# An earlier start behind four normalisations of a two-layer decoder step: what moves on each engine

## The chip, the core and the metric

The kernel runs on one core of one Trainium2 chip, as a single program. The metric is the device time of one execution in microseconds (us). Engines and the names that the profile gives them: TensorE (PE for its matmuls, PEld for its weight loads), VectorE (DVE), ScalarE (ACT), GpSimd (POOL) and SyncE (SP), which issues the weight transfers. The engines run side by side, each in its own program order, and wait for each other by semaphores only.

## The reference, cut to what matters

256 prompt tokens and 8 sample tokens go through two layers together, so that every operand has 264 columns. All sub-layers have the same frame:

```python
x = LayerNorm(alpha * x + (1 + gate) * sublayer(x * (1 + scale) + shift))
# layer 0: q, k, v = h @ w_qkv; attention; @ w_o      then  (silu(h @ w1) * (h @ w3)) @ w2
# layer 1: a, g = h @ w_pw1 + b; u = a * sigmoid(g); depthwise conv over 31 taps;
#          silu(layernorm(.)) @ w_pw2 + b             then  top-2-of-8 mixture of experts
```

`LayerNorm` takes mean and variance over the 1024 channels. `scale`, `shift` and `gate` are rows of `silu(c) @ ada_w + ada_b`, one vector per sequence. Everything is float32.

## The kernel before, in words

Activations lie transposed: 128 partitions hold 128 channels, eight chunks of them (`KC` = 8) make the 1024 channels, and the columns are the 264 tokens. A float32 product is made of three passes: both operands are cut into a high part (`w_hi`, `h_hi`, a cast to the rounded type `fp32r` on ScalarE) and a low part (`w_lo`, `h_lo`, the difference, on VectorE), and TensorE adds hi*hi, hi*lo and lo*hi.

**Weights.** SyncE loads blocks of 1 MB into a ring of seven slots, in the order of the list `stream`. A block of 1024 rows by 256 columns is split in two units; ScalarE casts a unit (line 982), VectorE subtracts (line 1245). There is room for two split blocks (`SPLITS` = 4 units), so a block is split only when the block two places before it has been used: `freed` holds the count of filled banks that says so (line 473). `split_behind(name)` splits the block two places behind `name`; the place of the call in VectorE's and ScalarE's program decides when.

**Dense stages.** `dense` (line 459) takes one block after the other. Each block makes two groups of 24 matmuls (8 chunks by 3 passes), one group in one bank of 512 floats. Six banks go round: `group()` lets TensorE wait until the group six places before it has been drained by VectorE (`psum_drained`). The stages are q/k/v (12 blocks "qkv"), the output product ("wo", 4), "f1"/"f3" (11 pairs), "f2", "p1"/"p1g" (4 pairs) and "p2" (4). Behind them the mixture of experts runs through its own loops.

**Norms.** `norm` of TensorE, ScalarE and VectorE together: VectorE adds the residual chunk by chunk, TensorE sums the chunks into the mean, VectorE centres in four parts (line 1326), ScalarE squares each part (line 969), TensorE sums the squares, ScalarE takes the root (line 971) and VectorE the reciprocal (line 1329). Norms 0 (behind wo), 1 (behind f2), 2 (inside the convolution module), 3 (behind p2) and 4 (at the end). `norm_modulate` then makes the next operand `hT` in two halves of four chunks, ScalarE casts each half to `h_hi` (line 995) and VectorE subtracts `h_lo` (line 1256). After both, `h_ready` is announced, and the next dense stage waits for that.

**Beside the norms.** TensorE is given other work while it waits: in norms 0, 1 and 2 it multiplies four pieces of `ada_w` each (`ada_rows`, line 485), whose four groups are the four that stand in front of the next stage's groups in the round of banks. VectorE copies them out (`ada_row`, line 1212) behind `h_ready` (behind `conv_ready` in norm 2), and TensorE turns them into columns behind the first blocks of the next stage (`ada_turn`, line 497).

**First stage.** For qkv VectorE splits block 0, makes `hT` (`modulate`), and then splits block 1.

## Time and profile before

| what | value |
|---|---|
| time of the runs | 2003.96 us median of 3 (2002.76 to 2003.96) |
| the profiled execution | 2008.72 us, its span 2007.0 us |
| TensorE busy | 1831.6 us (91%) |
| VectorE busy | 1524.6 us (76%) |
| ScalarE busy | 1168.8 us (58%) |
| DMA | 579 MB, mean 289 GB/s |

The span runs from the first to the last instruction; the time of the execution has 1.7 us around it. The first 755 us of the span are the stages that the change touches, the rest is the mixture of experts and norm 4. A busy share is an average over stages with different limits: what counts for the change are the places where TensorE stands still at a stage's border.

### The profile page before, as it was taken

How to read it: one execution, taken by the hardware profiler on the slowest of the kernel's cores; microseconds unless marked ns; L12 is line 12 of the kernel's file. 1: busy time of each engine (PE TensorE's matmuls, PEld its weight loads, DVE VectorE, ACT ScalarE, POOL GpSimd, SP SyncE). 2: the span in 40 equal slices, each digit the busy share in tenths (PEclk: the TensorE clock that was granted, in tenths of full speed). 3: DMA queues.
4: the chain of work that ended last, by engine and by line, in shares of the span. 5: the costliest groups of instructions: out<-in, count | busy, mean ns of one | idle time of the engine just before them, and what ended most of it. 6: DMA issues, size and time to landing. Idle time of an engine off the chain costs nothing.

```text
span 2007.0 us, 27233 instructions
## 1 busy us (share of the span) xinstructions
PE 1831.6 (91%) x10086; PEld 1471.7 (73%) x10086; DVE 1524.6 (76%) x1604; ACT 1168.8 (58%) x1030; POOL 18.1 (1%) x73
## 2 busy tenths in 40 slices
PE   5999778999899878998999999999999999999997
PEld 2974457999788766676676767676688787887885
DVE  2567736555679758989899898989888788887884
ACT  1321213443345327888877887877767767676773
POOL 2000000000000000000000000000000000000000
PEclk8985778999989888999999999999999999999998
DMA  9747677555743416999999999999999899898980
GB/s 299 230 149 238 245 251 252 168 174 182 240 141 104 175 39 245 382 385 388 388 390 394 380 388 386 381 386 390 387 330 366 324 338 370 304 357 337 329 314 22
DMA packets 246105, 579.27 MB, mean 289 GB/s; under 512 B 10478, under 2 KB 122550, under 8 KB 246013
## 3 DMA queue, kind: packets, MB, share of 16 engines
q1 hardware_dynamic: 245005, 573.98, 78.7%
q0 software_dynamic: 1024, 4.25, 0.6%
q8 instruction: 51, 0.84, 0.2%
q14 instruction: 25, 0.20, 0.0%
HBM read 574.79 MB, written 4.35 MB: 289 GB/s over the span
## 4 chain that ended last, share of the span: by engine, by line
PE 58%; DVE 16%; issue 7%; ACT 5%; DVEq 1%; DMA 0%; ACTq 0%; SPq 0%; PEldq 0%
PE banks L861 17%; PE banks L468 12%; DVE w_lo L1622 12%; PE banks L849 11%; PE banks L819 4%; ACT w_hi L1092 4%; PE banks L678 3%; PE banks L699 2%; PE banks L805 1%; PE banks L765 1%; PE banks L783 1%; PE banks L540 1%; PE banks L517 1%; PE banks L829 1%; PE banks L497 1%
## 5 line engine op out<-in xcount | busy, mean ns | idle before, releaser
L1622 DVE TENSOR_TENSOR w_lo<-ring,w_hi 128x2048 fp32r<-128x2048 f32 x420 | 945.6, 2288 | 146.0 <-ACT w_hi L1092 146.0
L1092 ACT CAST w_hi<-ring 128x2048 fp32r<-128x2048 f32 x420 | 798.7, 1912 | 265.9 <-PE banks L861 169.1
L861 PE MATMUL banks<-w_hi,x_s 128*128 128x512 f32 x672 | 279.3, 416 | 45.5 <-DVE w_lo L1622 39.6
L849 PE MATMUL banks<-w_hi,g_buf 128*128 128x512 f32 x784 | 282.5, 401 | 5.2 <-DVE w_lo L1622 2.8
L861 PE MATMUL banks<-w_hi,x_m 128*128 128x512 f32 x896 | 283.1, 392 | 2.3 <-DVE w_lo L1622 2.3
L468 PE MATMUL banks<-h_hi,w_hi 128*128 128x264 f32 x800 | 238.1, 298 | 29.5 <-DVEq L430 29.5
L861 PE MATMUL banks<-w_lo,x_s 128*128 128x512 f32 x672 | 264.7, 394 | 0.0
L982 ACT CAST w_hi<-ring 128x1024 fp32r<-128x1024 f32 x124 | 121.5, 1031 | 198.3 <-PE banks L468 93.0
L468 PE MATMUL banks<-h_lo,w_hi 128*128 128x264 f32 x800 | 233.9, 292 | 0.0
L468 PE MATMUL banks<-h_hi,w_lo 128*128 128x264 f32 x800 | 233.4, 292 | 0.0
L1245 DVE TENSOR_TENSOR w_lo<-ring,w_hi 128x1024 fp32r<-128x1024 f32 x124 | 143.9, 1204 | 106.0 <-ACT w_hi L982 105.2
L849 PE MATMUL banks<-w_lo,g_buf 128*128 128x512 f32 x560 | 218.9, 391 | 0.0
L861 PEld LDWEIGHTS banks<-w_hi,x_s 128*128 128x128 f32 x672 | 127.0, 189 | 113.7 <-DVE w_lo L1622 86.4
L861 PEld LDWEIGHTS banks<-w_hi,x_m 128*128 128x128 f32 x896 | 168.2, 188 | 37.6 <-DVE w_lo L1622 2.7
L849 PEld LDWEIGHTS banks<-w_hi,g_buf 128*128 128x128 f32 x784 | 147.2, 188 | 53.1 <-DVE w_lo L1622 22.4
L468 PEld LDWEIGHTS banks<-h_hi,w_hi 128*128 128x128 f32 x800 | 158.4, 198 | 31.5 <-DVEq L430 31.2
L861 PE MATMUL banks<-w_lo,x_m 128*128 128x512 f32 x448 | 174.5, 389 | 0.0
L468 PEld LDWEIGHTS banks<-h_lo,w_hi 128*128 128x128 f32 x800 | 158.5, 198 | 0.4
L468 PEld LDWEIGHTS banks<-h_hi,w_lo 128*128 128x128 f32 x800 | 157.4, 197 | 0.0
L861 PEld LDWEIGHTS banks<-w_lo,x_s 128*128 128x128 f32 x672 | 127.3, 189 | 23.7
L849 PEld LDWEIGHTS banks<-w_lo,g_buf 128*128 128x128 f32 x560 | 105.3, 188 | 19.8
L861 PEld LDWEIGHTS banks<-w_lo,x_m 128*128 128x128 f32 x448 | 84.1, 188 | 17.1
(347 smaller groups left out, 1912.8 us busy)
## 6 DMA issues: line engine op xcount, KB each, us to landing
ring<-in_moe_w_dram SPq DMA_DIRECT2D x420, 1024.0 KB, 7.4
ring<-in_ada_w_dram SPq DMA_DIRECT2D x48, 1024.0 KB, 5.9
ring<-in_ffn_w_dram SPq DMA_DIRECT2D x30, 1024.0 KB, 5.5
ring<-in_attn_w_qkv_dram SPq DMA_DIRECT2D x12, 1024.0 KB, 11.9
ring<-in_conv_w_pw_dram SPq DMA_DIRECT2D x12, 1024.0 KB, 9.7
ring<-in_cache_k_dram SPq DMA_DIRECT2D x16, 512.0 KB, 6.0
ring<-in_cache_v_dram SPq DMA_DIRECT2D x16, 512.0 KB, 7.5
ring<-in_attn_w_o_dram SPq DMA_DIRECT2D x4, 1024.0 KB, 8.5
```

What stands on the lines that cost most here:

```text
L468: mm = pe.matmul(bk[:, 0:T], w, x[:, k, :], start=(k == 0 and i == 0), stop=(k == KC - 1 and i == 2))
L497: mm = pe.matmul(bk[:, 9 * m:9 * m + 9], arow[i % 4][:, m * P:(m + 1) * P], fold, start=True, stop=True)
L517: mm = pe.matmul(stat[:, 0:T], mean_w[:, :], z[:, c, :], start=(c == 0), stop=(c == KC - 1))
L678: mm = pe.matmul(two[m][:, 0:T], w, x[:, g, :], start=(g == 0 and i == 0), stop=(g == FM - 1 and i == 2))
L699: mm = pe.matmul(bk[:, 0:TP], dw_diag[:, (c * PE_TAPS + i) % DIAGS, :], up[:, c, j:j + TP], start=(i == 0), stop=(i == PE_TAPS - 1))
L819: mm = pe.matmul(t_b[:, b, i * SMALL:(i + 1) * SMALL], h_rows[:, b, i * P:(i + 1) * P], joint[:, :], start=True, stop=True)
L849: mm = pe.matmul(out_b[:, b, :], g, y, start=(p == 0 and t == 0 and i == 0), stop=(p == NCH - 1 and t == 2 * last + 1 and i == len(g_passe ...
L861: mm = pe.matmul(bk[:, b, :], x, y, start=(k == 0 and i == 0), stop=(k == KC - 1 and i == len(x_passes(k, hi, lo)) - 1), skip_group_check= ...
L982: act.copy(w_hi[:, (q * UNITS + u) % SPLITS, 0:e - o], ring[:, n % RING, o:e]).then_inc(ev("w_hi_ready"), 1)
L1092: act.copy(w_unit(n)[0], ring[:, pos_of(n), :]).then_inc(ev("moe_hi_ready"), 1)
L1245: dve.tensor_tensor(w_lo[:, i, 0:e - o], ring[:, n % RING, o:e], w_hi[:, i, 0:e - o].bitcast(F32), ALU.subtract).then_inc(ev("w_lo_ready"), 1)
L1622: dve.tensor_tensor(lo, ring[:, pos_of(n), :], hi.bitcast(F32), ALU.subtract).then_inc(ev("moe_lo_ready"), 1)
```

## The change

Four edits, in TensorE's, ScalarE's and VectorE's programs. The numbers of lines in the diff are those of the two files; the rows named L487, L1267, L1278, L1234, L1349 and so on are the changed file's names for what is L468, L1245, L1256, L1212, L1326 before.

1. A new function `dense_halves` multiplies two blocks at once: it waits for both split blocks, takes all four groups, and then does the first four chunks for all groups, and the last four for all groups. It waits for `h_lo_ready` of each half in place of `h_ready`. It is used for qkv 0 and 1, f1/f3 0, p1/p1g 0 and p2 0 and 1. Both blocks count as used when all four groups are filled.
2. In norms 0 and 1 the last split in front of the centring is moved behind the centring on VectorE (`split_behind(behind)` in `rstd_ready`).
3. ScalarE takes a root of one column (`warm`) in front of the squares of every norm, which places the root's table load there.
4. In `modulate` (qkv) the low part of half 0 is made inside half 1, as `norm_modulate` does already.

```diff
+            def dense_halves(i, slots, x_hi, x_lo, behind=None):
+                for s in slots:
+                    wait_split(s)
+                groups = [(s, m, group((s, m))) for s in slots for m in range(2)]
+                for half in range(2):
+                    pe.wait_ge(ev("h_lo_ready"), 2 * i + half + 1)
+                    for s, m, bk in groups:
+                        for k in range(4 * half, 4 * half + 4):
+                            hi, lo = halves(s, k, m)
+                            for n, (w, x) in enumerate(((hi, x_hi), (hi, x_lo), (lo, x_hi))):
+                                mm = pe.matmul(bk[:, 0:T], w, x[:, k, :], start=(k == 0 and n == 0),
+                                               stop=(k == KC - 1 and n == 2), skip_group_check=True)
+                        if half:
+                            filled(mm)
+                for s in slots:
+                    freed[split_no[s]] = (psum_filled, len(order))
+                if behind is not None:
+                    for s, m, _bk in groups:
+                        behind(s, m)
...
-            pe.wait_ge(ev("h_ready"), 1)
-            dense([("qkv", j) for j in range(12)], h_hi, h_lo)
+            dense_halves(0, [("qkv", j) for j in range(2)], h_hi, h_lo)
+            dense([("qkv", j) for j in range(2, 12)], h_hi, h_lo)
...
-            pe.wait_ge(ev("h_ready"), 2)
-            for j in range(FF // 256):
+            dense_halves(1, [("f1", 0), ("f3", 0)], h_hi, h_lo)
+            while pending:
+                ada_turn()
+            for j in range(1, FF // 256):
                 dense([("f1", j), ("f3", j)], h_hi, h_lo)
...
-                dense([("p1", j), ("p1g", j)], h_hi, h_lo)
-                if j == 0:
+                if j:
+                    dense([("p1", j), ("p1g", j)], h_hi, h_lo)
+                else:
+                    dense_halves(2, [("p1", j), ("p1g", j)], h_hi, h_lo)
...
-            pe.wait_ge(ev("conv_ready"), 2)
             behind = mean_behind(3, zT)
-            dense([("p2", 0)], h_hi, h_lo, behind)
+            dense_halves(3, [("p2", 0), ("p2", 1)], h_hi, h_lo, behind)
             while pending:
                 ada_turn()
-            dense([("p2", j) for j in range(1, 4)], h_hi, h_lo, behind)
+            dense([("p2", j) for j in range(2, 4)], h_hi, h_lo, behind)
...
             def norm(i, z, s):
+                act.activation(warm[:, 0:1], eps_t[:, 0:1], ACT.Sqrt)
                 for part in range(PARTS):
...
             def low_halves(i, half):
-                step(dve.tensor_tensor(h_lo[:, c, :], hT[:, c, :], h_hi[:, c, :].bitcast(F32), ALU.subtract))
+                step(dve.tensor_tensor(h_lo[:, c, :], hT[:, c, :], h_hi[:, c, :].bitcast(F32), ALU.subtract), ev("h_lo_ready"))
...
             def modulate(i, layer, k):
                 for half in range(2):
                     s = slice(4 * half, 4 * half + 4)
+                    if half:
+                        low_halves(i, 0)
...
-                for half in range(2):
-                    low_halves(i, half)
+                low_halves(i, 1)
                 announce("h_ready")
...
-            def rstd_ready(i, z):
+            def rstd_ready(i, z, behind=None):
...
+                if behind is not None:
+                    split_behind(behind)
                 dve.wait_ge(ev("ln_std_ready"), i + 1)
...
-                if c % 2:
+                if c % 2 and c < KC - 1:
                     split_behind(("wo", c // 2))
-            norm_modulate(0, zT[:, :, :], PRM_LNG, PRM_LNB, 1, beside_norm[0])
+            norm_modulate(0, zT[:, :, :], PRM_LNG, PRM_LNB, 1, beside_norm[0], ("wo", 3))
...
-                split_behind(("f2", cb, 2))
-            norm_modulate(1, zT[:, :, :], PRM_LNG + KC, PRM_LNB + KC, 2, beside_norm[1])
+                if cb < 3:
+                    split_behind(("f2", cb, 2))
+            norm_modulate(1, zT[:, :, :], PRM_LNG + KC, PRM_LNB + KC, 2, beside_norm[1], ("f2", 3, 2))
...
-                if c == 1:
+                if c == 3:
                     while pending:
                         ada_turn()
```

**VectorE, the first stage** (`hT` and `h_lo` for qkv; the two `w_lo` rows at the end are block 1). In the words behind each row stand the semaphores it waits for. Before:

```order
L1245 TENSOR_TENSOR w_lo<-ring,w_hi 128x1024 [waits w_hi_ready] x2
L1264 TENSOR_SCALAR hT<-xT,adaT 128x256 [waits psum_drained]
...
L1268 TENSOR_TENSOR hT<-t,adaT 128x4x8 [waits vector_step]
L1264 TENSOR_SCALAR hT<-xT,adaT 128x256 [waits vector_step]
...
L1256 TENSOR_TENSOR h_lo<-hT,h_hi 128x1056 [waits vector_step,h_hi_ready]
L1256 TENSOR_TENSOR h_lo<-hT,h_hi 128x1056 [waits h_hi_ready]
L1245 TENSOR_TENSOR w_lo<-ring,w_hi 128x1024 [waits vector_step,w_hi_ready]
```

Now:

```order
L1267 TENSOR_TENSOR w_lo<-ring,w_hi 128x1024 [waits w_hi_ready] x2
L1288 TENSOR_SCALAR hT<-xT,adaT 128x256 [waits psum_drained]
...
L1278 TENSOR_TENSOR h_lo<-hT,h_hi 128x1056 [waits vector_step,h_hi_ready]
L1288 TENSOR_SCALAR hT<-xT,adaT 128x256 x4
...
L1278 TENSOR_TENSOR h_lo<-hT,h_hi 128x1056 [waits vector_step,h_hi_ready]
L1267 TENSOR_TENSOR w_lo<-ring,w_hi 128x1024 [waits h_lo_ready,w_hi_ready]
L1267 TENSOR_TENSOR w_lo<-ring,w_hi 128x1024 [waits w_hi_ready]
```

The low part of half 0 now stands in front of the second half's work; block 1's split is still last.

**VectorE, norm 0** (from the last residual chunk to the copies of the `ada_w` rows). Before:

```order
L1317 TENSOR_TENSOR zT<-zT,t 128x8 [waits psum_drained,vector_step,ln_chunk_ready]
L1245 TENSOR_TENSOR w_lo<-ring,w_hi 128x1024 [waits w_hi_ready] x2
L1326 TENSOR_TENSOR zT<-zT,banks 128x528 [waits stats_filled,ln_chunk_ready]
L1326 TENSOR_TENSOR zT<-zT,banks 128x528 x3
L1329 RECIPROCAL rstd<-std 128x264 [waits ln_std_ready]
...
L1256 TENSOR_TENSOR h_lo<-hT,h_hi 128x1056 [waits vector_step,h_hi_ready]
L1212 COPY arow_sb<-banks 128x512 [waits vector_step,psum_filled]
L1212 COPY arow_sb<-banks 128x512 [waits psum_drained,psum_filled]
```

Now:

```order
L1340 TENSOR_TENSOR zT<-zT,t 128x8 [waits psum_drained,vector_step,ln_chunk_ready]
L1349 TENSOR_TENSOR zT<-zT,banks 128x528 [waits stats_filled,ln_chunk_ready]
L1349 TENSOR_TENSOR zT<-zT,banks 128x528 x3
L1267 TENSOR_TENSOR w_lo<-ring,w_hi 128x1024 [waits w_hi_ready] x2
L1354 RECIPROCAL rstd<-std 128x264 [waits ln_std_ready]
...
L1278 TENSOR_TENSOR h_lo<-hT,h_hi 128x1056 [waits vector_step,h_hi_ready]
L1234 COPY arow_sb<-banks 128x512 [waits h_lo_ready,psum_filled]
L1234 COPY arow_sb<-banks 128x512 [waits psum_drained,psum_filled]
```

The split is behind the centring; the copies of the `ada_w` rows stand behind the second `h_lo`, as before.

**TensorE, the start of f1/f3 0** (the row in front is the last of the `ada_w` rows). Before:

```order
L485 MATMUL banks<-ring,cT_sb 32x256 [waits slot2_loaded]
L485 MATMUL banks<-ring,cT_sb 32x256 x7
L468 MATMUL banks<-h_hi,w_hi 128x264 [waits psum_drained,w_lo_ready,h_ready]
...
L468 MATMUL banks<-h_hi,w_hi 128x264 [waits psum_drained]
...
L468 MATMUL banks<-h_hi,w_hi 128x264 [waits psum_drained,w_lo_ready]
```

Now:

```order
L507 MATMUL banks<-ring,cT_sb 32x256 [waits slot2_loaded]
L507 MATMUL banks<-ring,cT_sb 32x256 x7
L487 MATMUL banks<-h_hi,w_hi 128x264 [waits psum_drained,h_lo_ready,w_lo_ready]
L487 MATMUL banks<-h_lo,w_hi 128x264
...
L487 MATMUL banks<-h_hi,w_hi 128x264 [waits h_lo_ready]
```

The waits for drained banks, which stood in front of each of the four groups, stand in front of the very first matmul now; 48 matmuls later only the second half of `h_lo` is waited for.

## Rows read from the trace of the kernel before

**Rows 1.** The page's head: the span.

```profile
span 2007.0 us, 27233 instructions
```

**Rows 2.** TensorE's waits from 25 to 1999 us: for whom, total, times, longest.

```profile
PE banks L468 <- DVEq L430: 29.5, 5, 9.1
...
PE banks L642 <- DMA ring<-in_cache_v_dram: 5.2, 1, 5.2
...
PE banks L712 <- DMA arena<-in_state_conv_dram: 3.8, 1, 3.8
```

**Rows 3.** Timeline, first stage: start, duration, engine, line, tiles, [idle before <- releaser].

```profile
46.73 1.38 DVE L1264 TENSOR_SCALAR hT<-xT,adaT 128x256 f32<-128x256 f32 x4
...
48.52 1.07 ACT L995 CAST h_hi<-hT 128x1056 fp32r<-128x1056 f32 x1
...
50.44 2.43 DVE L1256 TENSOR_TENSOR h_lo<-hT,h_hi 128x1056 fp32r<-128x1056 f32 x2
52.98 0.29 PEld L468 LDWEIGHTS banks<-h_hi,w_hi 128*128 128x128 f32 x1 [9.17 <-DVEq L430]
```

**Rows 4.** Timeline of VectorE and ScalarE: splits of block qkv 1 and of a later one.

```profile
53.01 2.36 DVE L1245 TENSOR_TENSOR w_lo<-ring,w_hi 128x1024 fp32r<-128x1024 f32 x2
...
67.45 2.00 ACT L982 CAST w_hi<-ring 128x1024 fp32r<-128x1024 f32 x2 [3.79 <-PE banks L468]
68.53 2.36 DVE L1245 TENSOR_TENSOR w_lo<-ring,w_hi 128x1024 fp32r<-128x1024 f32 x2 [0.70 <-ACT w_hi L982]
```

**Rows 5.** Timeline, norm 0, from the last split to the root.

```profile
306.01 1.83 PE L517 MATMUL banks<-zT,mean_w 128*128 128x264 f32 x6
...
306.26 1.99 ACT L982 CAST w_hi<-ring 128x1024 fp32r<-128x1024 f32 x2 [4.70 <-PE banks L468]
...
309.62 2.54 DVE L1326 TENSOR_TENSOR zT<-zT,banks 128x528 f32<-128x528 f32 x4
310.35 2.49 ACT L969 ACTIVATE arena<-zT 128x528 f32<-128x528 f32 x4 [2.09 <-DVE zT L1326]
...
312.86 1.28 ACT L971 ACT_TABLE_LOAD   x1
...
314.91 0.48 ACT L971 ACTIVATE std<-banks,eps_t 128x264 f32<-128x264 f32 x1 [0.77 <-PE banks L540]
```

**Rows 6.** Timeline, mixture of experts: another table load and a small activation behind it.

```profile
745.62 1.28 ACT L1102 ACT_TABLE_LOAD   x1
...
746.91 0.20 ACT L1102 ACTIVATE edif<-dif 128x3 f32<-128x3 f32 x1
```

**Rows 7.** Timeline, norm 0, the low parts and the copies behind them.

```profile
321.77 1.26 DVE L1256 TENSOR_TENSOR h_lo<-hT,h_hi 128x1056 fp32r<-128x1056 f32 x1
...
325.85 1.26 DVE L1256 TENSOR_TENSOR h_lo<-hT,h_hi 128x1056 fp32r<-128x1056 f32 x1 [1.19 <-ACT h_hi L995]
...
327.25 1.53 DVE L1212 COPY arow_sb<-banks 128x512 f32<-128x512 f32 x2
```

**Rows 8.** The chain that ended last, in order of time, behind norm 0.

```profile
327.22 13.84 PE banks L468 x96
341.06 3.47 PE banks L497 x32
```

**Rows 9.** Timeline of VectorE: one product of the f stage; the copies in norm 2.

```profile
339.04 0.42 DVE L1510 TENSOR_TENSOR arena<-arena,banks 128x264 f32<-128x264 f32 x1
...
685.43 1.53 DVE L1212 COPY arow_sb<-banks 128x512 f32<-128x512 f32 x2
```

**Rows 10.** Stretches: start:end, us, busy of each engine, granted PE clock, DMA share, GB/s.

```profile
344.60:348.60 4.00, 4.00 (x22) 4.00 (x22) 1.90 (x7) 0.00 (x0) 0.00 (x0) 0.58 0.51 146
...
562.80:566.70 3.90, 0.11 (x1) 0.00 (x0) 2.93 (x5) 3.75 (x5) 0.00 (x0) 1.00 0.39 98
570.30:577.10 6.80, 6.80 (x34) 6.80 (x33) 1.83 (x7) 0.42 (x2) 0.00 (x0) 0.50 0.58 188
577.10:581.00 3.90, 3.90 (x20) 3.90 (x20) 3.68 (x9) 0.00 (x0) 0.00 (x0) 0.53 0.02 4
```

More of the change, by code:

```diff
@@ L132, in build @@
         std = sb("std", [P, T])
+        warm = sb("warm", [P, 1])
         rstd = sb("rstd", [P, T])
@@ L657, in _ @@
             norm(0, zT, sq, beside=beside_norm[0])
-            pe.wait_ge(ev("h_ready"), 2)
-            for j in range(FF // 256):
+            dense_halves(1, [("f1", 0), ("f3", 0)], h_hi, h_lo)
+            while pending:
+                ada_turn()
+            for j in range(1, FF // 256):
                 dense([("f1", j), ("f3", j)], h_hi, h_lo)
-                if j == 0:
-                    while pending:
-                        ada_turn()
             behind = mean_behind(1, zT)
@@ L689, in _ @@
             norm(1, zT, sq, beside=beside_norm[1])
-            pe.wait_ge(ev("h_ready"), 3)
             def taps(c):
@@ L705, in _ @@
             for j in range(4):
-                dense([("p1", j), ("p1g", j)], h_hi, h_lo)
-                if j == 0:
+                if j:
+                    dense([("p1", j), ("p1g", j)], h_hi, h_lo)
+                else:
+                    dense_halves(2, [("p1", j), ("p1g", j)], h_hi, h_lo)
                     pe.wait_ge(ev("state_loaded"), 32)
@@ L1281, in fuse, with norm_modulate @@
                 step(dve.tensor_tensor(fuse_b[:, :, :], fuse_b[:, :, :], shift, ALU.add))
-            def norm_modulate(n, z, g, b, i, beside=()):
-                rstd_ready(n, z)
+            def norm_modulate(n, z, g, b, i, beside=(), behind=None):
+                rstd_ready(n, z, behind)
                 for half in range(2):
```

## The prediction

> **What bounds the kernel now.** I read the page's head first: a span of 2007.0 us [rows 1], inside an execution of 2008.72 us. Then the waits of TensorE, because it is the engine that is busy for 91%: between its work it waited 29.5 us in five places for the next dense operand, the longest 9.1 us [rows 2]. Those are the borders that the change aims at. Each is read in the timeline. The chain of waits shows what comes behind a border: 96 matmuls in 13.84 us without a hole, and four column turns in 3.47 us [rows 8], with the next block right behind them. So inside the stages TensorE is the bound, and what a border gains or loses runs through to the end; I found no later stage that waits for a fixed moment. For the change three things must be followed at each border: when the first matmul may start, when the two blocks' room is free again, and what the clock does.
>
> **First stage (qkv): later start.** In the changed order the first matmul needs both blocks' low parts, and block 1's subtractions still stand behind the making of the operand. Half of `hT` is made from 46.73 to the cast at 48.52, 1.79 us; the cast takes 1.07, a low part 2.43/2 = 1.22 [rows 3]. Now VectorE must wait for the cast before it goes on: low part 0 is done at 48.52 + 1.07 + 0.03 + 1.22 = 50.84, half 1 is made by 52.63, its cast by 53.70, low part 1 by 54.95. Then come block 1's subtractions, 0.14 + 2.36 us [rows 4]: 57.45, and TensorE starts at 57.5 and not at 52.98 [rows 3]. That is **+4.5**. The early low part helps nobody, because the weights come last.
>
> **First stage: an empty room.** `dense_halves` frees both blocks only when all four groups are full, so that block 2 can be split only then. Before, block 0's room came free 48 matmuls earlier and this was hidden. A split takes 67.45 to 68.53 + 2.36 = 70.89, 3.44 us [rows 4]; with an estimated 0.3 for the hand-over at both ends TensorE stands still for **+3.75**. Ends: 3.44 with no hand-over, and 4.2 if VectorE's copies of the groups come in between.
>
> **The clock behind such a hole.** The granted clock was still 1.00 in a wait of 3.9 us and 0.50 in the work behind it; that is the 2.4 and the 1.2 GHz level [rows 10]. Behind the column turns of norm 0 it was 0.58 over 4.0 us: 84% of them at the lower level, half of which is lost, 1.7 us [rows 10]. In the hole of 3.75 us I expect the same: **+1.7** (ends 0 and 2.0). Together +9.95 for qkv.
>
> **Norm 0: the squares.** Without the split in front, the centring could start some 1.7 us earlier, when the mean is there (the sums end at 306.01 + 1.83 = 307.84, the centring started at 309.62 [rows 5]). But ScalarE is late then. Its last cast ends at 308.25, the table load takes 1.28, and the small root, which the trace does not have, lies between 0 and the 0.48 of the whole root [rows 5]; I take the 0.20 of the nearest small activation [rows 6]. The squares start at 309.75 and not at 310.35: **-0.6** (ends -0.8 and -0.3). The load as such wins nothing: after it ScalarE waited another 0.77 us for TensorE's sums [rows 5], and that pause is the same in all norms. In norms 2, 3 and 4 nothing stands in front of the centring, ScalarE has time for the load: 0. VectorE's moved 2.36 us end near 313, before the root at 314.3: hidden; without that cover they would cost up to 2.36. They free a ring slot 3 us later, so that the last pieces of `ada_w` land later; TensorE has some 7 us of waiting to take them.
>
> The Trainium skill, "ScalarE: Activation LUTs", section "What ACT_TABLE_LOAD costs", gives a load of 1283 ns and a drain of about 1380 ns more, 2.66 us a switch. The load agrees with the trace (1.28), the drain does not: the next activation starts at 746.91, right behind the load that ends at 746.90 [rows 6]. By the page's figure the squares of norms 0 and 1 would start 1.38 us later than I say.
>
> **Norms 0, 1 and 2: the start behind the copies.** The early start needs the first low part alone, at 323.03 and not 327.11 in norm 0 [rows 7]. It will not come. All four groups are taken in front of the first matmul, there are six banks, and the four groups before them are the `ada_w` rows. Group 4 needs the bank of the second row, and VectorE copies the rows behind the second low part: two copies, 1.53 us, from 327.25 [rows 7]. So TensorE starts at 327.25 + 1.53 + 0.07 = 328.85, or 328.25 with the 0.6 gained, against 327.22 [rows 8]: **+1.05**. Norm 1 has the same copies and the same order in front of them, so the same gain: **+1.05**. Part of that could hide in the wait of 3.8 us for the conv state [rows 2], but VectorE's four splits behind p1g 0 move with the end of the blocks and hold its copies for the next turns; I count it whole (ends 0 and 1.05). Norm 2 has the copies [rows 9] and no gain: **+1.6**. For p2 the room is no trouble: two mean sums and four column turns fill the 3.7 us in which block 2 is split. Ends for that: 0 and +0.7.
>
> **f1/f3 behind norm 0.** The pair ends 13.84 us after its start, as before. Before, f1 1 was split while f3 0 was multiplied, and only the turns (3.47) stood between [rows 8]. Now ScalarE casts f1 1 from the end on; after 0.2 + 3.44 us VectorE has its low part, and only behind it stand the two products of 0.42 [rows 9], after which the four banks are handed back: about 4.7 us. Turns 3 and 4 need these banks. So f1 1 starts 4.7 + 3.47/2 = 6.5 us behind the end at full clock; the clock will have fallen by then, which makes the two turns 3.5 us long: 8.2 us, against 3.47, **+4.75**. The low level then lasts some 4 us from the start of the full matmuls, as it did behind the turns of norm 1 (0.53 over 3.9 us [rows 10]), and costs 2.0 in place of 1.7: **+0.3**. Ends for the two: +3.0 and +5.5. In p1 the next splits waited for both blocks anyway: 0.
>
> **The sum.** 4.5 + 3.75 + 1.7 + 1.05 + 4.75 + 0.3 + 1.05 + 1.6 = 18.7 us. The profiled execution took 2008.72, and would be 2027.4; the median of the runs is 2003.96, 4.8 below it, and the steps are waits between engines, the same in both. So 2003.96 + 18.7 = **2022.7 us**.
>
> **The rivals.**
> - *The clock stays up* in the qkv hole and in turns 3 and 4. For: a fall needs its moment, and the hole is no longer than the one in which it had not yet fallen. Against: it fell right behind it. Without 1.7 + 1.75 + 0.3 it is +14.95: 2018.9.
> - *Later waits swallow a part.* The wait of 5.2 us for the V pages [rows 2] could be a transfer that comes at its own time; then a later qkv stage costs that much less: +13.5, 2017.5. Against: the pages are asked for when ring slots come free, and these move along.
> - *The table switch holds ScalarE 2.66 us*, as the activations in front of the squares would then: 2 x 1.38 more, +21.5, 2025.4. Against it stands the row above. The page named above is its source.
> - *Faster: TensorE starts with the first low part everywhere.* Place: the first matmul of the four stages. Start at 50.9 in qkv (-2.0), 4.1 + 0.6 earlier in norms 0 and 1, 3.1 in norm 2: -14.5; the holes stay (3.75 + 1.7 + 3.0 = +8.45): -6, 1998. It decides once three of the four starts come at the first `h_lo`. For: that is how the code reads. Against: the waits for block 1 and for the banks in the order of the instructions.
> - *Nothing to be seen*: losses at the holes are hidden by slack that I missed, and the sum is under 4 us.
>
> **Chances and range.** The forecast 0.60, with a range of its own from 2020 to 2026; clock up 0.17; swallowed 0.08; table switch 0.05; more than summed (copies in the holes, 2027 to 2030) 0.04; faster 0.03; no change 0.03. The range from 2016 to 2027 takes in the first four with most of their spread. A measurement of this kernel tells about 0.2% (4 us) from no change. Faster 0.03, same 0.03, slower 0.94.
>
> **What would show it.** In the changed profile: first matmul of qkv at about 57.5; a hole of 3.5 to 4 us in TensorE between qkv 1 and qkv 2, then matmuls at double spacing; squares of norm 0 starting 0.6 us earlier against the last cast; the first matmul behind norms 0, 1 and 2 right behind the second copy of an `ada_w` row; a hole between the second and third turn behind f1/f3 0, and the next block 8 us behind the pair. I am wrong if one of these starts follows the first low part, if a stage's end catches up what its start lost, or if the attention stage takes less time than before.

## The result and the profile after

The changed kernel took **2032.04 us** (median of 4 runs, 2030.67 to 2036.5), the kernel before 2003.96 beside it: a ratio of 1.0133, 95% interval 1.0117 to 1.0149, which is +26.7 us (23.4 to 29.9). It is slower, as forecast, but the forecast of 2022.7 us is 9.3 us too low and its range ended at 2027.

The profiled execution took 2031.49 us. Its head answers to [rows 1]:

```profile
span 2029.7 us, 27245 instructions
```

TensorE's waits of the changed kernel (for whom, total, times, longest) answer to [rows 2]:

```profile
PE banks L487 <- DVE arow_sb L1234: 17.4, 3, 8.0
PE banks L487 <- DVE w_lo L1267: 13.3, 1, 13.3
...
PE banks L664 <- DMA ring<-in_cache_v_dram: 5.0, 1, 5.0
...
PE banks L469 <- DVE w_lo L1267: 3.6, 1, 3.6
...
PE banks L519 <- DVEq L416: 2.8, 1, 2.8
```

The 29.5 us in five places have become 17.4 behind the copies of `ada_w` rows (three places: norms 0, 1, 2), 13.3 in front of qkv behind block 1's subtractions, and two new holes, 3.6 and 2.8. No start stands behind a low part. TensorE's waits for pieces of `ada_w` grew from 3.4 to 10.0 us, but they fall into time in which it would wait anyway: in norm 0 the last piece is done at 325.54, three microseconds before its row can be copied.

**First stage**, timeline of the changed kernel, against [rows 3, 4]:

```profile
49.94 1.07 ACT L1017 CAST h_hi<-hT 128x1056 fp32r<-128x1056 f32 x1 [1.68 <-DVEq L431]
...
56.60 2.36 DVE L1267 TENSOR_TENSOR w_lo<-ring,w_hi 128x1024 fp32r<-128x1024 f32 x2
59.03 0.29 PEld L487 LDWEIGHTS banks<-h_hi,w_hi 128*128 128x128 f32 x1 [13.39 <-DVE w_lo L1267]
...
73.04 3.89 ACT L1004 CAST w_hi<-ring 128x1024 fp32r<-128x1024 f32 x4 [17.88 <-PE banks L487]
74.12 2.36 DVE L1267 TENSOR_TENSOR w_lo<-ring,w_hi 128x1024 fp32r<-128x1024 f32 x2 [3.63 <-ACT w_hi L1004]
...
76.53 0.39 PE L469 MATMUL banks<-h_hi,w_hi 128*128 128x264 f32 x1 [3.59 <-DVE w_lo L1267]
```

From the first `h_hi` to TensorE's first load it is 9.09 us against 4.46, and block 2 comes 3.59 us after the pair. The stretch behind that hole (columns as in [rows 10]) has the lower clock level again:

```profile
76.90:80.40 3.50, 3.50 (x20) 3.50 (x19) 2.52 (x3) 0.03 (x1) 0.00 (x0) 0.53 0.76 257
```

**Norm 0**, timeline, against [rows 5]:

```profile
307.91 1.82 PE L539 MATMUL banks<-zT,mean_w 128*128 128x264 f32 x6
308.17 1.99 ACT L1004 CAST w_hi<-ring 128x1024 fp32r<-128x1024 f32 x2 [4.70 <-PE banks L469]
...
309.85 2.55 DVE L1349 TENSOR_TENSOR zT<-zT,banks 128x528 f32<-128x528 f32 x4 [0.87 <-PE banks L539]
310.18 1.28 ACT L987 ACT_TABLE_LOAD   x1
311.47 0.20 ACT L987 ACTIVATE warm<-eps_t 128x1 f32<-128x1 f32 x1
311.58 2.23 ACT L991 ACTIVATE arena<-zT 128x528 f32<-128x528 f32 x4
312.31 2.35 DVE L1267 TENSOR_TENSOR w_lo<-ring,w_hi 128x1024 fp32r<-128x1024 f32 x2
316.13 0.48 ACT L993 ACTIVATE std<-banks,eps_t 128x264 f32<-128x264 f32 x1 [2.31 <-PE banks L562]
```

From the start of the last cast to the start of the squares: 3.41 us against 4.09. The centring starts right behind the mean, but ScalarE is late by the load. The moved subtractions end at 314.66, before the root at 316.13.

**The start and the hole behind norm 0**, against [rows 7, 8]:

```profile
327.13 1.26 DVE L1278 TENSOR_TENSOR h_lo<-hT,h_hi 128x1056 fp32r<-128x1056 f32 x1 [1.19 <-ACT h_hi L1017]
328.54 1.53 DVE L1234 COPY arow_sb<-banks 128x512 f32<-128x512 f32 x2
330.32 0.56 PE L487 MATMUL banks<-h_hi,w_hi 128*128 128x264 f32 x1 [4.78 <-DVE arow_sb L1234]
...
343.33 1.85 PE L519 MATMUL banks<-fold,arow_sb 128*128 128x9 f32 x16
343.58 1.99 ACT L1004 CAST w_hi<-ring 128x1024 fp32r<-128x1024 f32 x2 [2.43 <-PE banks L487]
344.77 2.36 DVE L1267 TENSOR_TENSOR w_lo<-ring,w_hi 128x1024 fp32r<-128x1024 f32 x2 [10.16 <-ACT w_hi L1004]
347.05 0.76 DVE L1535 TENSOR_TENSOR arena<-arena,banks 128x264 f32<-128x264 f32 x2
348.01 3.55 PE L519 MATMUL banks<-fold,arena 128*128 128x9 f32 x16 [2.83 <-DVEq L416]
...
351.41 0.57 PE L469 MATMUL banks<-h_hi,w_hi 128*128 128x264 f32 x1
```

All of that is near what was forecast. What was not is the mixture of experts, whose code the change does not touch. From its first cast of weights to the squares of norm 4 it takes 1246.84 us (765.22 to 2012.06), before 1235.66 (753.46 to 1989.12). In each matmul there the operand of 128 columns that is loaded first (`x_s` or `x_m`, the experts' tokens, or `g_buf`, their gated product) is called stationary, and the weights of 512 columns (`w_hi`, `w_lo`) are the moving operand. These matmuls before (duration in ns: min/median/max, first and last start in us):

```profile
L861 PE MATMUL banks<-w_hi,x_m x896: 387/389/587, 1455.3 to 1950.4; 128*128 128x512 f32 x180
L861 PE MATMUL banks<-w_lo,x_s x672: 387/389/628, 766.7 to 1433.8; 128*128 128x512 f32 x168
...
L849 PE MATMUL banks<-w_hi,g_buf x784: 387/389/504, 812.4 to 1973.3; 128*128 128x512 f32 x196
```

and after:

```profile
L882 PE MATMUL banks<-w_hi,x_m x896: 387/396/588, 1468.1 to 1973.1; 128*128 128x512 f32 x180
L882 PE MATMUL banks<-w_lo,x_s x672: 387/395/628, 778.5 to 1446.6; 128*128 128x512 f32 x168
...
L870 PE MATMUL banks<-w_hi,g_buf x784: 392/396/502, 824.3 to 1996.4; 128*128 128x512 f32 x196
```

The same instructions are some 6 ns longer (only those of `w_hi` with `x_s`, whose median was 393 before, by 3). The clock is not the cause, it is 1.00 in both. The experts' stretch, before:

```profile
770.00:1985.00 1215.00, 1153.70 (x5265) 899.68 (x5265) 1040.96 (x648) 912.02 (x588) 0.00 (x0) 1.00 0.94 354
```

and after:

```profile
781.00:2008.00 1227.00, 1170.97 (x5265) 901.27 (x5264) 1043.32 (x649) 914.40 (x590) 0.00 (x0) 1.00 0.93 351
```

5265 matmuls (some 4000 of them of this kind) are busy for 17.3 us more, the stretch is 12 us longer, and VectorE, ScalarE and the weight loads are busy for as long as before within 2.5 us. Up to the first `x_m` matmul the stage costs only +1.0 us, because TensorE waits for VectorE's splits there and its waits shrink instead (41.9 us to 39.4, the row L861 or L882 behind `w_lo`); behind it TensorE is the bound and it costs +10.1. In the chain of waits the same 72 matmuls stand with 16.38 us before and 16.79 after.

### The profile page after: what moved, and what is told of

Its sections match the earlier page's. It is cut to its first block, busy times and chain, and to the rows that moved or that the text cites. A ratio compares the mean times of both kernels' runs of the same rounds, so it can differ in the third digit from the quotient of the medians.

```text
span 2029.7 us, 27245 instructions
## 1 busy us (share of the span) xinstructions
PE 1843.8 (91%) x10086; PEld 1472.5 (73%) x10086; DVE 1525.7 (75%) x1604; ACT 1169.0 (58%) x1035; POOL 18.2 (1%) x73
## 4 chain that ended last, share of the span: by engine, by line
PE 58%; DVE 16%; issue 7%; ACT 5%; DVEq 1%; DMA 0%; ACTq 0%; SPq 0%; PEldq 0%
PE banks L882 17%; DVE w_lo L1648 11%; PE banks L870 11%; PE banks L469 10%; PE banks L840 4%; ACT w_hi L1114 3%; PE banks L699 3%; PE banks L719 2%; PE banks L487 2%; PE banks L826 1%; PE banks L786 1%; PE banks L804 1%; PE banks L562 1%; PE banks L539 1%; PE banks L519 1%
## 5 line engine op out<-in xcount | busy, mean ns | idle before, releaser
L882 PE MATMUL banks<-w_hi,x_s 128*128 128x512 f32 x672 | 281.0, 418 | 41.7 <-DVE w_lo L1648 37.2
L882 PE MATMUL banks<-w_hi,x_m 128*128 128x512 f32 x896 | 288.6, 398 | 2.3 <-DVE w_lo L1648 2.3
L882 PE MATMUL banks<-w_lo,x_s 128*128 128x512 f32 x672 | 267.1, 397 | 0.0
L1267 DVE TENSOR_TENSOR w_lo<-ring,w_hi 128x1024 fp32r<-128x1024 f32 x124 | 143.8, 1204 | 118.2 <-ACT w_hi L1004 117.5
L882 PEld LDWEIGHTS banks<-w_hi,x_s 128*128 128x128 f32 x672 | 127.0, 189 | 111.8 <-DVE w_lo L1648 82.6
L469 PE MATMUL banks<-h_hi,w_hi 128*128 128x264 f32 x672 | 197.7, 294 | 4.2 <-DVE w_lo L1267 3.6
L882 PEld LDWEIGHTS banks<-w_hi,x_m 128*128 128x128 f32 x896 | 168.3, 188 | 42.9 <-DVE w_lo L1648 2.7
L469 PE MATMUL banks<-h_lo,w_hi 128*128 128x264 f32 x672 | 194.7, 290 | 0.0
L469 PE MATMUL banks<-h_hi,w_lo 128*128 128x264 f32 x672 | 194.5, 289 | 0.0
L882 PE MATMUL banks<-w_lo,x_m 128*128 128x512 f32 x448 | 177.1, 395 | 0.0
L882 PEld LDWEIGHTS banks<-w_lo,x_s 128*128 128x128 f32 x672 | 127.4, 190 | 25.1
L469 PEld LDWEIGHTS banks<-h_hi,w_hi 128*128 128x128 f32 x672 | 131.3, 195 | 4.8 <-DVE w_lo L1267 3.8
L469 PEld LDWEIGHTS banks<-h_lo,w_hi 128*128 128x128 f32 x672 | 131.2, 195 | 0.3
L469 PEld LDWEIGHTS banks<-h_hi,w_lo 128*128 128x128 f32 x672 | 130.5, 194 | 0.0
L882 PEld LDWEIGHTS banks<-w_lo,x_m 128*128 128x128 f32 x448 | 84.2, 188 | 19.9
```

The lines of the kernel that those rows point to most:

```text
L469: mm = pe.matmul(bk[:, 0:T], w, x[:, k, :], start=(k == 0 and i == 0), stop=(k == KC - 1 and i == 2))
L882: mm = pe.matmul(bk[:, b, :], x, y, start=(k == 0 and i == 0), stop=(k == KC - 1 and i == len(x_passes(k, hi, lo)) - 1), skip_group_check= ...
L1267: dve.tensor_tensor(w_lo[:, i, 0:e - o], ring[:, n % RING, o:e], w_hi[:, i, 0:e - o].bitcast(F32), ALU.subtract).then_inc(ev("w_lo_ready"), 1)
```

## The experiments

The suspect for the experts was the one thing that the change does to them: `warm`, a new tile of 4 bytes a partition (the line that allocates it is not in the excerpt of the diff above; e2's diff takes it out again). In the program's addresses, which no trace shows, it takes 32 bytes, and all tiles allocated later lie 32 bytes higher, among them `x_s`, `x_m` and `g_buf`. The weights `w_hi` and `w_lo` lie in front of it and stay. Ratios are to the kernel before beside the same runs, with 95% intervals; in us they are taken of its medians there (2004.65 for the first four, 2005.64 for e5 to e8, 2005.23 for e9 to e12, 2002.4 for the last three).

| run | what it is | us, runs | ratio |
|---|---|---|---|
| e1_pad32 | before + unused 4-byte tile | 2018.25, 6 | 1.0061 [1.0048, 1.0074] |
| e2_after_inplace | the change, no tile moved | 2023.63, 6 | 1.0090 [1.0075, 1.0105] |
| e3_no_qkv | e2, qkv as before | 2014.12, 5 | 1.0044 [1.0030, 1.0057] |
| e4_split_only | only the moved splits | 2002.61, 12 | 0.9990 [0.9979, 1.0001] |
| e5_pad64 | before + two such tiles | 2018.48, 4 | 1.0064 [1.0042, 1.0085] |
| e6_pad_x | before, 32 B at the experts' tiles alone | 2015.95, 5 | 1.0049 [1.0032, 1.0066] |
| e7_pad_behind | the 32 B behind them | 2005.75, 1 | |
| e8_split_warm | e4 + the early root | 2005.58, 12 | 0.9996 [0.9983, 1.0009] |
| e9_lazy_own | halves with late banks, own release | 1995.24, 6 | 0.9955 [0.9939, 0.9970] |
| e10_lazy_only | e9, common release | 2000.51, 10 | 0.9978 [0.9967, 0.9990] |
| e11_no_f1 | e2, f1/f3 0 as before | 2018.11, 4 | 1.0058 [1.0038, 1.0078] |
| e12_pad128 | 128 B in front of `x_s` | 2014.04, 1 | |
| e13_pad256 | 256 B in front of `x_s` | 2003.89, 1 | |
| e14_pad_w128 | 128 B in front of `w_hi` | 2005.78, 1 | |
| e15_pad_g128 | 128 B in front of `g_buf` | 2013.23, 1 | |

### The tile

**e1_pad32** puts the tile, unused, into the kernel before; **e2_after_inplace** keeps the whole change but lets the small root write into a free column of `prm`.

```diff
         std = sb("std", [P, T])
+        pad = sb("pad", [P, 1])
```
```diff
-        warm = sb("warm", [P, 1])
+        warm = prm[:, 508:509]
```

> The kernel before with one unused tile of 4 bytes per partition where the change has its tile warm; the tiles behind it then lie 32 bytes further on. Layout theory: the matmuls of the mixture of experts go from a median of 389 to 396 ns, as in the changed kernel, and the time rises by about 11 us (2015). Rival (the mixture of experts was slower for a cause of the run, or of the new order in front of it): the time stays within 3 us of before and the median at 389 ns.

> The changed kernel with the one-column root written into a free column of the parameter tile, so that no tile moves; nothing else differs. Layout theory: median of the expert matmuls back at 389 ns, the time about 11 us below the changed kernel, 12 to 17 us above before (2016 to 2021). Rival (the order causes the slower experts): as the changed kernel, 28 us above before.

The unused tile alone makes the kernel 12.2 us slower (9.6 to 14.8), and the experts' stage 1248.55 us long. Without the shift the whole change costs 18.0 us (15.0 to 21.0), and the experts are back at 1235.56. That is the missing part and the forecast part, each by itself; they add up to 30.2, against 26.7 (23.4 to 29.9) measured. For e1 I had expected about 11; for e2 12 to 17, which is a microsecond below what came.

**Which tiles, and which distance.** e5 adds two tiles; e6 and e7 put the 32 bytes at the experts' tiles, in front of all three or behind them; e12 and e13 widen e6's gap to 128 and 256 bytes.

```diff
+        pad = sb("pad", [P, 8], at=moe)     # e6; e12: [P, 32], e13: [P, 64]
         x_s = sb("x_s", [P, KC, 2, SMALL], F32R, at=moe)
...
         g_buf = sb("g_buf", [P, 2, SLOTW], F32R, at=moe)
+        pad = sb("pad", [P, 8], at=moe)     # e7 alone, in place of the first
```

> The kernel before with two unused tiles of 4 bytes: each takes 32 bytes, so that everything behind them lies 64 bytes further on. If the expert matmuls care where their operand lies within 64 bytes, it is as before: median 389 ns, time within 3 us of before. If they care for the tile's being there, or for 128 bytes and more: 395 ns or over and 10 to 14 us slower.

> The kernel before with 32 bytes put in front of x_s, so that only the experts' tiles (x_s, x_m, g_buf and those behind) move by 32 bytes, and all others stay. If the place of the experts' operands is the cause: 395 ns or more and 10 to 14 us slower, all of it in the mixture of experts. If a tile in front of them is (rstd, the arena): as before.

> The 32 bytes put behind g_buf: x_s, x_m and g_buf, the stationary operands of the expert matmuls, stay on their 64-byte places, and h_rows, the selectors and all others move. If the stationary operands alone count: median 389 ns and the experts' stage 1236 us, as before. If h_rows or another of the moved tiles counts: the 8 to 12 us are there again.

> The kernel before with 128 bytes in front of x_s, so that the experts' tiles move by 128 bytes (e6 moved them by 32). If the stationary operands want to begin on a multiple of 128 bytes: median 389 ns, experts' stage 1236 us. If it is their place as such, or multiples of 256 with an offset of 128: 395 ns or more and 1247 us.

> The kernel before with 256 bytes in front of x_s. If only the place within 256 bytes counts (before, x_s, x_m and g_buf lie 128 bytes past a multiple of 256): median 389 ns, experts' stage 1236 us. If the period is 512 bytes or more, or any move slows: 392 ns or more and 1245 us or more.

Experts' stage: e5 1250.27, e6 1246.83, e7 1235.74, e12 1245.94, e13 1235.79 us. So it is the place of `x_s`, `x_m` and `g_buf` that counts, and not the count of tiles or those behind. 32, 64 and 128 bytes are slow, 256 are as none. The matmuls of `g_buf` in e12 and in e13:

```profile
L850 PE MATMUL banks<-w_hi,g_buf x784: 388/395/506, 807.6 to 1980.2; 128*128 128x512 f32 x196
...
L850 PE MATMUL banks<-w_hi,g_buf x784: 387/389/504, 807.4 to 1968.5; 128*128 128x512 f32 x196
```

**Absolute or relative?** **e14_pad_w128** moves the weights and the token operands together by 128 bytes, **e15_pad_g128** moves `g_buf` alone.

```diff
+        pad = sb("pad", [P, 32])            # e14
         w_hi_all = sb("w_hi", [P, WBUF * SLOTW], F32R)
...
+        pad = sb("pad", [P, 32], at=moe)    # e15 alone
         g_buf = sb("g_buf", [P, 2, SLOTW], F32R, at=moe)
```

> 128 bytes in front of w_hi, so that the moving operands (w_hi, w_lo) and the stationary ones (x_s, x_m, g_buf) move together by 128. If their distance from each other counts: median 389 ns and 1236 us, as before. If the absolute place of the stationary operand counts: as e12, 392 ns or more and 1245 us.

> 128 bytes between x_m and g_buf. If each matmul is slowed by the place of its own stationary operand: the matmuls of w1 and w3 (x_s, x_m) keep 389 ns and those of w2 (g_buf) go to 393, the stage by about 4 us. If the slowing is one for the whole stage: both groups alike.

With all moved together (e14) the stage takes 1235.63 us (of its six groups of matmuls only `w_lo` with `x_s` is off, 393 ns in place of 389; why is open), and the same matmuls:

```profile
L850 PE MATMUL banks<-w_hi,g_buf x784: 387/389/504, 809.4 to 1970.4; 128*128 128x512 f32 x196
```

With `g_buf` alone moved (e15):

```profile
L862 PE MATMUL banks<-w_hi,x_m x896: 387/389/587, 1457.2 to 1954.6; 128*128 128x512 f32 x180
...
L850 PE MATMUL banks<-w_hi,g_buf x784: 390/396/506, 813.4 to 1977.9; 128*128 128x512 f32 x196
```

Only the matmuls that load the moved tile are slow, and the stage takes 1239.18, +3.5. (The run as a whole is longer by more, because its attention stage took 170.6 us and e13's 164.3: more on that below.) So the time of these matmuls depends on the distance in a partition between their two operands: fast where it is what it was or 256 bytes more, slow at 32, 64 or 128 bytes more. Nor is it shown for other shapes: the 528 matmuls of f2, 264 columns wide, whose moving operand `g_hi_f` or `g_lo_f` also lies behind the tile (its chunks are 1056 bytes apart, so they stand at many distances in both), are busy for 150.2 us before and 150.2 in e1.

### The borders

**e3_no_qkv** and **e11_no_f1** take the new order out of one stage each, both on top of e2.

```diff
-            dense_halves(0, [("qkv", j) for j in range(2)], h_hi, h_lo)
-            dense([("qkv", j) for j in range(2, 12)], h_hi, h_lo)
+            pe.wait_ge(ev("h_ready"), 1)
+            dense([("qkv", j) for j in range(12)], h_hi, h_lo)
```
```diff
-            dense_halves(1, [("f1", 0), ("f3", 0)], h_hi, h_lo)
+            pe.wait_ge(ev("h_ready"), 2)
+            dense([("f1", 0), ("f3", 0)], h_hi, h_lo)
```

(e3 also makes `h_lo` of half 0 at its old place.)

> As e2, but the qkv stage as before (dense, low parts behind both halves). If the start of qkv and the hole behind it cost what they cost at their place (11 us at the end of the qkv stage) and the attention stage's later catching up is tied to them: about 2 us below e2. If the catching up has a cause of its own (the clock's phase, the layout of the attention tiles): about 11 us below e2, or the attention stage is as long as before.

> The change in place (no tile moved) with f1/f3 0 as before. My sum: the later start of 1.05 and the hole with its low clock, 5.05, go away: 6.1 us below e2 (2017). Rival (later stages catch up what f1/f3 lost): within 2 us of e2.

Taking the order out of qkv gives back 9.5 us between the medians of e2 and e3 (9.95 in the sum): the second of the two cases that I had named for e3. Taking it out of f1/f3 0 gives 5.5 (1.05 + 4.75 + 0.3 = 6.1 forecast; e11 was timed in another group of runs than e2). By the intervals of the ratios each of the two differences is uncertain by 4 to 5 us, so they agree with the sum but don't prove its terms; the rows do that below.

**e4_split_only** keeps of the change only the splits behind the centring, **e8_split_warm** that and the early root (in place).

```diff
 # e8; e4 is without this line
+                act.activation(warm[:, 0:1], eps_t[:, 0:1], ACT.Sqrt)
```

> The kernel before with nothing but the weight subtractions of norms 0 and 1 moved behind the centring. The centring starts when the mean is there: 1.6 us a norm, -3.2 us in all (2000.8). Rival: the subtractions hold up the reciprocal, or the ring slots freed later hold up the ada_w pieces: no change or slower.

> As e4 (subtractions behind the centring), and the one-column root in front of the squares of every norm, in place, so that no tile moves. My sum: in norms 0 and 1 the squares wait for ScalarE's table load and start 1.0 us later than in e4, nothing in the other norms: +2.0 us against e4. Rival (the early table load gains 1.28 us a norm): 2 to 6 us below e4.

The squares start 2.42 us behind the last cast in e4, 3.41 in e8, as in the changed kernel. Norm 0 of e4, where the table load is behind the squares again:

```profile
302.97 1.83 PE L539 MATMUL banks<-zT,mean_w 128*128 128x264 f32 x6
...
304.91 2.55 DVE L1349 TENSOR_TENSOR zT<-zT,banks 128x528 f32<-128x528 f32 x4 [0.88 <-PE banks L539]
305.65 2.48 ACT L992 ACTIVATE arena<-zT 128x528 f32<-128x528 f32 x4 [0.43 <-DVE zT L1349]
...
308.15 1.28 ACT L994 ACT_TABLE_LOAD   x1
```

So the moved split is worth 1.67 us in norm 0 (1.54 in norm 1) and the early load takes 0.99 of that back. As whole kernels neither can be told from the kernel before: -2.0 us (-4.2 to +0.2, forecast -3.2) and -0.8 (-3.4 to +1.8).

**e9_lazy_own** asks what the order by halves would give without its two holds: each group takes its bank in front of its own first matmul, and each block is handed back with its own two groups. It is built on e4 (no early root) and leaves qkv as before. **e10_lazy_only** has the late banks but hands both blocks back together.

```diff
-                groups = [(s, m, group((s, m))) for s in slots for m in range(2)]
+                groups = [(s, m) for s in slots for m in range(2)]
+                bank = {}
...
+                        if not half:
+                            bank[s, m] = group((s, m))
+                        bk = bank[s, m]
...
-                    freed[split_no[s]] = (psum_filled, len(order))
+                    freed[split_no[s]] = (psum_filled, where[s, 1] + 1)     # e9 only
```

> The early start with its two hindrances taken away: each group asks for its bank right in front of its own first matmul, and a block counts as used when its own two groups are full. qkv as before, subtractions behind the centring, no early table load, no new tile. If the bank order and the common release were what the change lost at norms 0 to 2: the first matmul comes right behind the first low part (4.1 us before the second in norms 0 and 1, 3.1 in norm 2), f1/f3 win 4.2, p2 3.1, p1 between 0 and 4.2 since it waits for the conv state: 7 to 11 us below e4, 1991 to 1996. Rival (TensorE gains nothing by half an operand, since it runs at the lower clock then): within 3 us of e4.

> As e9, but both blocks are released together, as in the change. If the hole behind f1/f3 0 comes from that release: next block 8 us behind the pair and not 4.5, 3 to 5 us above e9. Rival (the hole comes from the banks taken at once): as e9.

e9 is faster than both kernels: 1995.24 us, -9.0 (-12.2 to -6.0). Norm 0 in its timeline:

```profile
312.79 1.07 ACT L1020 CAST h_hi<-hT 128x1056 fp32r<-128x1056 f32 x1 [5.04 <-DVEq L431]
...
314.14 1.26 DVE L1281 TENSOR_TENSOR h_lo<-hT,h_hi 128x1056 fp32r<-128x1056 f32 x1
315.10 1.94 PE L511 MATMUL banks<-ring,cT_sb 128*32 128x256 f32 x16 [1.85 <-DMA ring<-in_ada_w_dram]
...
316.97 0.59 PE L491 MATMUL banks<-h_hi,w_hi 128*128 128x264 f32 x1
...
334.41 0.57 PE L469 MATMUL banks<-h_hi,w_hi 128*128 128x264 f32 x1
```

Now the first matmul does come before the second low part, 4.18 us behind the first cast against 6.79 before. It is the last piece of `ada_w` that holds it, not the low part, which ends at 315.40. The next block follows 17.44 us after the start, about as before (327.22 to 344.39, 17.17): with its own release the hole is gone. In e10 it is there, the third turn waits again:

```profile
334.94 0.69 DVE arena L1537 x2
335.65 0.03 DVEq L416
335.82 3.56 PE banks L523 x16
```

(the chain of waits of e10). The block after the pair starts at 339.37, 8.1 us behind the pair's end. The hole costs 3.2 us from the squares of norm 0 to those of norm 1 in the two profiles, and 5.3 us between the medians (3 to 5 expected). Most of e9's gain over e4 lies in p2: from the squares of norm 2 to those of norm 3 it takes 46.32 us, e4 52.67, before 51.97. There e9's first matmul comes 13.10 us behind the squares and e4's 16.05, and the clock does the rest. In e9 TensorE had waited 3.25 us and the clock stayed up; in e4 it had waited 6.21, and its matmuls ran at the 1.2 GHz level for 6 us. The stage in e9 and in e4 (columns as in [rows 10]):

```profile
658.80:705.00 46.20, 40.97 (x364) 35.90 (x356) 28.57 (x58) 15.74 (x21) 0.42 (x1) 1.00 0.66 231
...
661.30:714.00 52.70, 45.02 (x368) 40.09 (x356) 28.97 (x58) 15.80 (x22) 0.45 (x1) 0.87 0.57 203
```

Behind the turns of norm 0 it is the other way round: e9's blocks start 3.1 us earlier than e4's, but the granted clock is 0.78 in their first 10 us where e4 has 1.00, which is worth 2.2 us, and only 1.0 us is left at norm 1. In p1 the earlier start gained nothing: TensorE then waits for the conv state,

```profile
PE banks L738 <- DMA arena<-in_state_conv_dram: 7.2, 1, 7.2
```

which it did for 3.8 us before [rows 2] and 4.6 in e4. So e9's time of 1995.24 lies in the range that I had expected (1991 to 1996), but by luck: the f stage gave 1.0 us and not 4.2, p1 lost 1.6, and p2 gave 6.35 and not 3.1.

## Why the prediction was wrong

**The step that failed** is the sum: it has no term for the new tile `warm`. I said that the first 755 us are the stages that the change touches, took the mixture of experts behind them at +0 without a reason, and never asked where the tile puts what lies behind it. It costs 11.2 us of the profile, 12.2 as an experiment; with it the sum is 18.7 + 11.2 = 29.9, inside the interval of +23.4 to +29.9 at its upper end.

**The terms that stood in the sum held**, up to a microsecond. e2, the change without the shift, measures 18.0 us (15.0 to 21.0) against 18.7; that this is so close is in part luck, since the terms below add up to 19.6 in the profile. One by one, forecast and changed kernel's profile:

| term | forecast | measured |
|---|---|---|
| qkv, first `h_hi` to start | +4.5 | 9.09 - 4.46 = +4.6 |
| hole behind the pair | +3.75 | 3.59 |
| clock behind it | +1.7 | 3.50 us at 0.53: 1.65 |
| squares of norm 0 | -0.6 | -0.68 |
| norm 0's squares to norm 1's | +1.05 + 0.6 + 4.75 + 0.3 - 0.6 = +6.1 | 227.96 - 221.84 = +6.1 |
| norm 1's squares to norm 2's | +1.05 + 0.6 = +1.65 | 139.71 - 137.16 = +2.55 |
| norm 2's squares to norm 3's | +1.6 | 53.81 - 51.97 = +1.8 |

The 0.9 us that norm 1's squares to norm 2's are over the forecast are the clock again: in the second stretch of the convolution's matmuls, behind a wait of 3.5 us, it was 0.87 where it had been 1.00 behind a wait of 3.3, and they took 13.15 us and not 11.47, while the dense pairs in front of them took 0.6 less.

The first matmul of qkv is at 59.06 and not at 57.5. 1.4 of this was there before the change's first step (`h_hi` at 49.94 and not 48.52); in e2 it starts at 57.49, as forecast. The hole behind f1/f3 0 is as described: the block after the pair is 351.41 - 343.33 = 8.1 us behind its end, 8.2 forecast. And behind norms 0, 1 and 2 TensorE started behind the second copy.

**The rivals.** *The clock stays up*: it did not. *The table switch at 2.66 us*: the small root starts at 311.47, 0.01 us behind the load's end at 311.46, the cast in front of the load had ended at 310.16 and the load begins at 310.18, and e8 shows the same (308.84 + 1.28, then 310.13), so no drain is seen beside a load. The Trainium skill, "ScalarE: Activation LUTs", section "What ACT_TABLE_LOAD costs", has a drain of about 1380 ns there; by an estimate with that figure the squares of norm 0 would have come 0.7 us later than before, and the measurement decides against it. *Faster, by starting with the first low part*: the waits that the prediction named against it are what held. For the banks e9 shows it, where p2 starts right behind the first low part once they are taken late; for block 1 in qkv the only sign is the row of 13.3 us behind `w_lo`, since no run splits block 1 earlier. *Nothing to be seen*: no.

*Later waits swallow a part*: the profile looks so, and one of my own signs of being wrong appeared. From the table load for attention's first exponentials to the first use of wo's blocks it took 170.76 us before and 161.68 after, which gives back 9.1 of the 11.0 us by which attention began later. It was not the V pages (5.2 and 5.0 us of wait). It was the clock. Before:

```profile
116.00:286.00 170.00, 139.56 (x799) 79.99 (x798) 108.28 (x220) 29.77 (x96) 2.59 (x4) 0.68 0.65 224
```

and after:

```profile
127.00:288.00 161.00, 128.73 (x800) 74.69 (x799) 108.26 (x220) 29.38 (x96) 2.60 (x4) 0.78 0.69 236
```

The same work, with a granted clock of 0.68 and 0.78. TensorE's busy time alone is 10.8 us shorter. This stage is 161.6 us in e2, 165.5 in e11, and in the 14 profiles whose qkv is as before 164.3 (e13) to 170.8 us, with a mean of 167.3 and no edit in it. The three with the late qkv have a mean of 162.9, so part of the gift may belong to the change. The medians show none: e2 against e3 has 9.5 us of qkv's 9.95, but with its 4 us of uncertainty. e2's profile was the fastest of its six runs (2018.75, median 2023.63), and the profile of before was 4.8 us above its median. So the two profiles are 22.8 us apart where the medians are 28.1 apart. What makes the clock take the one or the other course here is open, and so is how much of it qkv's later start earns. Open too is why the distance of two operands changes a matmul's time.

## What to carry to other kernels

A new tile, however small, is a change of every address behind it: place it last or in a free column, or list the addresses of TensorE's operands before and after, and compare the medians of unchanged matmuls first when a stage that nobody touched gets slower. An order that starts with half the operand brings only as much as its other waits allow: take banks and hand back blocks group by group, or the early start is paid for twice. And before two profiles are subtracted, see how far each stands from the median of its kernel.

## What the runs showed of the hardware

- A matmul of 128x128 by 128x512 (float32 in rounded form) had a median of 389 to 390 ns (393 for `w_hi` with `x_s`, and in e14 for `w_lo` with `x_s`) when stationary and moving operand were a multiple of 256 bytes apart in the partition by the program's addresses (before, e7, e13, e14), and 392 to 398 ns at 32, 64 or 128 bytes more (the changed kernel, e1, e5, e6, e12, e15's `g_buf`). In a run of such matmuls that is 16.38 against 16.79 us for 72. Granted clock (1.00) and load times (188 ns) were the same.
- An unused tile of 4 bytes a partition, which by the program's addresses moves the tiles behind it by 32 bytes, made the kernel 12.2 us slower (e1).
- In attention the granted clock was 0.68 in one profile and 0.78 in the other for the same instructions, which took 9 us less in the other.
- A hole of 3.59 us was followed by 3.5 us of matmuls at a granted 0.53, mostly the 1.2 GHz level. In norm 2 a wait of 3.25 us was followed by matmuls at 1.00 (e9), one of 6.21 us by 5 us at 0.50 (e4).
- A table load of 1.28 us is followed by the next activation within 0.01 us, also where that is the root for which it was loaded; the squares behind it needed no load of their own.
